# Nine run borders interleaved, and one weight conversion moved ahead, in a one-core two-model kernel

## The reference

```
h = rms_norm(x, g)
r, k, v, gate = (h + dx * mu[i]) @ w_in[i]          # i = 0..3, each 1024 x 1024
y = delta_rule_scan(r, decay, k, v, kk, a)          # state of 64 x 64 per head
x = x + (group_norm(y) + bonus) * silu(gate) @ w_out
x = x + sigmoid(rms_norm(x) @ w_gate0) * (p[0] @ w_proj0)
q, k, v, gate = rms_norm(x) @ da_w_in               # then softmax attention, 8 heads
x = x + (attention * silu(gate)) @ da_w_out
x = x + sigmoid(rms_norm(x) @ w_gate1) * (p[1] @ w_proj1)
b, c, xin, g = rms_norm(rms_norm(x)) @ w_in_a       # b * conv(c * xin) * silu(g)
x = x + conv_out @ w_out_a
...                                                 # stick-breaking attention, output norm
```

## Time and profile before

| what | value |
|---|---|
| median of the runs | 1260.31 us (1258.64 to 1261.17) |
| the profiled execution: its time, its span | 1260.45 us, 1258.7 us |
| TensorE matmuls busy | 1165.2 us, 93% |
| VectorE, ScalarE, GpSimd busy | 752.7, 617.9, 484.8 us |
| mean granted TensorE clock | 0.973 of full |

### The profile page before, as it was taken

The page is one execution under the profiler, slowest core; times in us unless marked ns, Lnnn a source line. Parts: engine busy times, 40 slices in busy tenths (PEclk is TensorE's granted clock), DMA queues, the critical chain, the costliest instruction groups (busy, mean ns, idle before and its releaser), DMA issues.

```text
span 1258.7 us, 19508 instructions
## 1 busy us (share of the span) xinstructions
PE 1165.2 (93%) x7570; PEld 901.6 (72%) x7570; DVE 752.7 (60%) x1179; ACT 617.9 (49%) x1018; POOL 484.8 (39%) x391
## 2 busy tenths in 40 slices
PE   5899899997886899899999998999999999999977
PEld 4665667676773687677777776777888888867656
DVE  4775996793556536566766656364285234567753
ACT  4667453633553336656656464364221244466655
POOL 1432334355760244323333334443444445532321
PEclk8999899998998899999999999999999999999988
DMA  6742245427005162221221222522333333222111
GB/s 235 251 113 67 68 102 149 131 88 194 12 4 172 34 191 85 84 67 56 77 67 55 67 84 68 165 86 69 99 100 90 96 100 101 84 76 60 52 33 67
DMA packets 198909, 119.49 MB, mean 95 GB/s; under 512 B 27741, under 2 KB 187174, under 8 KB 198566
## 3 DMA queue, kind: packets, MB, share of 16 engines
q1 hardware_dynamic: 197312, 116.08, 31.4%
q10 hardware_dynamic: 1510, 2.20, 0.5%
HBM read 103.06 MB, written 15.20 MB: 94 GB/s over the span
## 4 chain that ended last, share of the span: by engine, by line
PE 38%; issue 29%; POOL 15%; DVE 12%; ACT 2%; DMA 2%; SPq 0%; POOLq 0%; ACTq 0%; DVEq 0%
POOL b_w_lo L547 13%; PE banks L625 10%; PE banks L626 10%; PE banks L627 10%; DVE b_problems L2077 2%; DVE b_sum_squares L2075 1%; PE banks L1193 1%; DVE b_a_lo L1937 1%; PE banks L632 1%; PE banks L1221 1%; POOL b_sum_squares L592 1%; DVE b_sum_squares L2010 1%; DMA b_spread_heads<-spread_heads 1%; DVE b_suffix L2523 1%; POOL b_squares L584 1%
## 5 line engine op out<-in xcount | busy, mean ns | idle before, releaser
L547 POOL TENSOR_TENSOR b_w_lo<-b_w_raw,b_w_hi 128x512 fp32r<-128x512 f32 x320 | 428.9, 1361 | 717.3 <-ACT b_w_hi L1291 717.2
L625 PE MATMUL banks<-b_a_lo,b_w_hi 128*128 128x512 f32 x1280 | 525.0, 410 | 31.6 <-DVE b_a_lo L2190 12.7
L627 PE MATMUL banks<-b_a_hi,b_w_lo 128*128 128x512 f32 x1280 | 505.5, 395 | 0.0
L626 PE MATMUL banks<-b_a_hi,b_w_hi 128*128 128x512 f32 x1280 | 504.7, 394 | 0.0
L625 PEld LDWEIGHTS banks<-b_a_lo,b_w_hi 128*128 128x128 f32 x1280 | 243.8, 190 | 110.5 <-issue 26.1
L1291 ACT ACTIVATE b_w_hi<-b_w_raw 128x1024 fp32r<-128x1024 f32 x160 | 168.7, 1055 | 252.4 <-PE banks L627 247.0
L627 PEld LDWEIGHTS banks<-b_a_hi,b_w_lo 128*128 128x128 f32 x1280 | 243.7, 190 | 53.9
L626 PEld LDWEIGHTS banks<-b_a_hi,b_w_hi 128*128 128x128 f32 x1280 | 244.6, 191 | 44.6
L1682 ACT ACTIVATE b_exps<-banks,b_stats 128x128 f32<-128x128 f32 (+3 forms) x64 | 33.2, 524 | 60.1 <-DVE b_stats L2313 60.1
L1617 ACT ACTIVATE b_a_hi<-b_x_t,b_params 128x512 fp32r<-128x512 f32 x48 | 33.9, 719 | 54.7 <-DVE b_x_t L2198 54.2
L2198 DVE TENSOR_TENSOR b_x_t<-b_x_t,banks 128x512 f32<-128x512 f32 x32 | 21.9, 686 | 60.7 <-PE banks L627 60.7
(11 more groups left out here) (315 smaller groups left out, 1512.4 us busy)
## 6 DMA issues: line engine op xcount, KB each, us to landing
b_w_raw<-rw_w_in SPq DMA_DIRECT2D x32, 512.0 KB, 4.4
b_w_raw<-da_w_in SPq DMA_DIRECT2D x32, 512.0 KB, 4.0
b_w_raw<-w_in_a SPq DMA_DIRECT2D x32, 512.0 KB, 4.0
b_w_raw<-pe_w_gate SPq DMA_DIRECT2D x16, 512.0 KB, 4.1
d_ple<-b_ple_out SPq DMA_DIRECT2D x16, 256.0 KB, 4.9
b_w_raw<-rw_w_out SPq DMA_DIRECT2D x8, 512.0 KB, 6.6
b_ple_in<-d_ple SPq DMA_DIRECT2D x2, 2048.0 KB, 10.3
b_w_raw<-da_w_out SPq DMA_DIRECT2D x8, 512.0 KB, 4.0
```

The costliest lines, as they stand in the source:

```text
L547: m = pool.tensor_tensor(WLO[:, u % 2, ks], WRAW[:, u, ks], WHI[:, u % 2, ks].bitcast(F32), ALU.subtract)
L625: pe.matmul(dst, hi, a_lo[:, k_act, :], start=first, stop=False)
L626: pe.matmul(dst, hi, a_hi[:, k_act, :], start=False, stop=False)
L627: return pe.matmul(dst, lo, a_hi[:, k_act, :], start=False, stop=last)
```

## The change

At nine borders the order of TensorE's work is changed. Before, the first tile of a run is computed whole, then the second. After, the last `late` steps of the first tile stand behind the first `lead` steps of the second. What the second tile's first matmul waits for (`begin`) is waited for at its new place. The nine borders are v (late 4, lead 4), gate (2, 3), RWO (3, 5), PE0 (1, 2), DA (1, 2), DAO (2, 4), PE1 (1, 2), CC (1, 2) and CO (1, 2). Where there is a row norm, `sums` stays behind the first tile's last step and `spread` stays three steps behind `sums`. On ScalarE the high part of the third tile of DA, `hi(RUN_DA[0] + 2)`, is moved from ahead of the first rotation to ahead of the copy of `b_rstd`. No instruction is added or removed; VectorE's, GpSimd's and SyncE's programs are the same.

```
+        def rw_first_two(run, late, lead):
+            s = run * NT
+            rw_begin(s)
+            rw_part(s, 0, NT - late)
+            rw_begin(s + 1)
+            rw_part(s + 1, 0, lead)
+            rw_part(s, NT - late, NT)
...
+                rw_first_two(2, 4, 4)
...
+                rw_first_two(3, 2, 3)
...
+        def run_of(run, a0, buf, tiles=NT, norm=None, late=1, lead=2):
...
+            begin(0)
+            part(0, 0, NT - late)
+            begin(1)
+            part(1, 0, lead)
+            part(0, NT - late, NT)
+            if norm is not None:
+                norm[0]()
+                part(1, lead, lead + 3)
+                norm[1]()
+                part(1, lead + 3, NT)
...
+        run_of(RUN_RWO, A_RWO, 0, late=3, lead=5)
         run_of(RUN_PE0, A_PE0, 1, norm=norm_rows(16, 4))
...
+        DA_SWAPPED = {NT - 1: (1, 0), NT: (1, 1), NT + 1: (0, NT - 1)}
...
-        run_of(RUN_DAO, A_DAO, 1)
+        run_of(RUN_DAO, A_DAO, 1, late=2, lead=4)
...
         rows_root(3, TT)
+        hi(RUN_DA[0] + 2)
         keep_rstd(RB[:, :], 3, BANK[4])
...
-            if q == 1:
+            if q == 1 and p:
                 hi(g0 + 3 * p + 2)
```

More of the change, by code:

```diff
@@ L729, in rw_slot, with rw_part @@
             pe.wait_ge(sem(name), s - 3 - first if s >= 4 else s + 1)
-            for k in range(NT):
+        def rw_part(s, first, last, middle=None):
+            run, j = divmod(s, NT)
+            for k in range(first, last):
                 if j == 0:
                     pe.wait_ge(sem("act_ready"), A_K + NT * run + k + 1)
-                last = split_product(BANK[s % 4], s % 2, lambda w, k=k: w[:, k, :], k, k == 0, k == NT - 1)
+                m = split_product(BANK[s % 4], s % 2, lambda w, k=k: w[:, k, :], k, k == 0, k == NT - 1)
                 if j == NT - 1 and k < NT - 1:
-                    last.then_inc(sem("a_free"), 1)
+                    m.then_inc(sem("a_free"), 1)
                 if k == 3 and middle is not None:
                     middle()
-            last.then_inc(sem("mm_done"), 1)
+                if k == NT - 1:
+                    m.then_inc(sem("mm_done"), 1)
+        def rw_slot(s, middle=None):
+            rw_begin(s)
+            rw_part(s, 0, NT, middle)
+        def rw_first_two(run, late, lead):
+            s = run * NT
+            rw_begin(s)
+            rw_part(s, 0, NT - late)
+            rw_begin(s + 1)
+            rw_part(s + 1, 0, lead)
+            rw_part(s, NT - late, NT)
         low, up = slice(0, CH), slice(CH, P)
@@ L835, in _ @@
         for j in range(NT):
-            rw_slot(2 * NT + j)
+            if j == 0:
+                rw_first_two(2, 4, 4)
+            elif j == 1:
+                rw_part(2 * NT + 1, 4, NT)
+            else:
+                rw_slot(2 * NT + j)
             if j < 2:
@@ L848, in _ @@
         for j in range(NT):
-            rw_slot(3 * NT + j)
+            if j == 0:
+                rw_first_two(3, 2, 3)
+            elif j == 1:
+                rw_part(3 * NT + 1, 3, NT)
+            else:
+                rw_slot(3 * NT + j)
             if j == 0:
@@ L1012, in _ @@
             head_spread(BANK[4 + j % 4], SPREADHR2, RKC2, j).then_inc(sem("gn_bcast"), 1)
[L1013 to L1018, removed]
-            else:
[L1020 to L1035, removed]
+        def run_of(run, a0, buf, tiles=NT, norm=None, late=1, lead=2):
+            def begin(j):
+                pe.wait_ge(sem("lo_done"), run[0] + j + 1)
+                if run == RUN_DAO and j < 3:
+                    pe.wait_ge(sem("bank_free"), RUN_DAO[1] - (1 if j == 0 else 0))
+                else:
+                    pe.wait_ge(sem("bank_free"), run[1] + j - 3)
+            def part(j, first, last):
+                for k in range(first, last):
+                    if j == 0:
+                        pe.wait_ge(sem("act_ready"), a0 + k + 1)
+                    m = split_product(BANK[j % 4], (run[0] + j) % 2, lambda w, k=k: w[:, k, :], k, k == 0, k == NT - 1, buf)
+                    if k == NT - 1:
+                        m.then_inc(sem("mm_done"), 1)
+            begin(0)
[8 more added lines that the diff above has]
+                part(1, lead + 3, NT)
+            else:
+                part(1, lead, NT)
+            for j in range(2, tiles):
+                begin(j)
+                part(j, 0, NT)
```

9 lines of the change are left out of this document (4 added, 5 removed).

## The result

The changed kernel takes 1276.82 us, the median of four runs (1275.36 to 1280.79), against 1260.74 us before in the same session. The ratio is 1.0137, with a 95% interval of 1.0115 to 1.0160: slower by 1.4%, close to the forecast of 1274.0 us and well inside its range. The profiled execution took 1276.94 us with a span of 1275.2 us and a mean granted clock of 0.968.

What follows compares the result with a forecast made beforehand. TensorE is busy 93% of the span; after borders, later tiles wait for weights made from the first tile's end. 1260.45 + 7.4 (order) + 6.35 (clock) = 1274.2, forecast as 1274.0 us; range 1264 to 1281.

Steps and rivals of the forecast that it cites:

- the order's term: Delay from the reordering itself, border by border: PE0 +2.05, DAO +2.9, PE1 +2.1, CO +0.45, v -0.2; all borders +7.4 us.
- those on `sums`: Sign: `sums` of PE0 and PE1 start two steps later, behind a wait for the weights' low part (L547).
- on DAO's sixth step: Sign: DAO's sixth step is followed by 2 us idle for the weights' low part (L547).
- on the totals: Sign: TensorE's total waits for L547 grow by over 8 us while those for `b_a_lo` shrink.
- on the slow windows: Sign: the profile after has more windows at half clock.
- 3 to 4 us: Sign: the third tiles of RWO and DAO wait this long for the weights' low part (L547).
- Rival A: The waits move but the clock does not answer: only +7.4, 1267.7 us; chance 0.17.
- D: Rival: no change, delays at PE0, PE1, DAO absorbed by norm slack and the moved conversion; 1260 us, chance 0.05.
- C: Rival: faster, TensorE's own work sets the pace after a border, decided at RWO's and DAO's third tiles; 1252.6 us, chance 0.08.
- Net for the rotation, the rope and so `scores`: At DA: `sums` 0.65 later, conversion of 1.04 moved out from ahead of the rotation, net -0.4 us.
- it stays: At RWO: the way from first tile to third, 5.96 us, is unchanged; the border costs +0.5 us.
- CC's "0": At CC: the third tile still starts when its weights are ready, so 0 delay, with a wait of about 2.3 us.

Runs made afterwards that it cites:

- DAO alone: The kernel before with only DAO's border interleaved (late 2, lead 4): 1264.42 us, ratio 1.0032.
- RWO's shorter lead: The changed kernel with RWO at 3 late and 2 lead steps instead of 5 lead: 1274.09 us.
- hi first: In RWO and DAO, hi of the tile two on ahead of the residual wait: 1254.66 us on the kernel before, 1267.75 us on the changed kernel.
- the filled pauses: The changed kernel with unread matmuls in the waits at RWO, PE0, PE1, the scores and CC: 1268.63 us, ratio 1.0066.
- the one with the held high part: The changed kernel, where ScalarE makes the high part of DA's fifth tile only behind the first head's last rope addition: 1277.33 us.
- the two combined versions: The kernel before with hi first, RWO 3 late/2 lead, earlier high parts at PE, DA, CC: 1258.36 us; plus 20 unread matmuls: 1253.39 us.

## Why the prediction came out

The direction and the main mechanism were right: a later tile's weights hang on the first tile's end, and steps put between only delay that end. At PE0, DAO, PE1, CO and before RWO the order's term came within 0.2 us. Undoing PE0 and PE1, DAO alone and RWO's shorter lead show the mechanism from three sides; hi first shows that the pace was the chain and names its slack link. Of the signs named beforehand those on `sums`, on DAO's sixth step, on the totals and on the slow windows are in the profile after; the waits of 4.21 and 2.93 us ahead of RWO's and DAO's third tiles lie just outside the "3 to 4 us", and PE0's fourth tile waits 2.44 us instead of 1.11. Rival A (no clock) and D (no change) are out by the filled pauses and by DAO alone; C fell with 4.21 us of wait ahead of RWO's third tile.

Two steps failed, both for the same reason: they followed the moved work on its own chain and not what then runs beside it. The first is "Net for the rotation, the rope and so `scores`". It holds to the rope (-0.34 for -0.4). But the conversion moved on ScalarE also lets the conversions behind it, and so a GpSimd subtraction, come 0.5 us earlier against the rope, and VectorE's last addition meets it: +0.92 us. The second is RWO's "it stays", and CC's "0". From the first tile's residual addition to the third tile's start RWO took 428.47 - 422.82 = 5.65 us before and 429.22 - 423.08 = 6.14 us after, since VectorE's split of the second tile now delays the subtraction; the same cost CC 0.46 us.

The order term so was 9.1 for 7.4, with 0.4 more spread over the rest, and the clock term 7.0 for 6.35. The price of one stretch, 1.7 us, was near (1.5 to 1.6). That the clock's sum came out so near is luck: the three pauses counted by half (measured 2.43 to 2.63 us) all got a stretch, and DAO's, counted in full, none. The Trainium skill's page "TensorE: Matmul & The Clock Gate", section "HAM oscillation — how this bites in real kernels", has every long enough wait answered by the slow clock; five of six were so here, and DAO's wasn't. The sum by that rule, about 1278, lies nearer to 1276.8 than mine, but for no better reason: its clock term, 10.2, is 3.2 too large, and the order term in it is 2.1 too small.

## What to carry to other kernels

Work put into a wait is worth something only if what the wait holds up isn't also held up by what was moved; follow the first late thing behind the border (here the third tile's weights) back to where it starts, and shorten that chain instead. ScalarE's conversions in two runs, placed ahead of a wait that they don't need, gave 6 us, where nine reordered borders cost 16. When an instruction moves, follow also the engine that it feeds, and look for what that one now runs beside.

## What the runs showed of the hardware

The same pause doesn't get the same clock: 2.57 us ahead of DA's third tile was followed by 1.00 before, and by 0.50 with hi first (timeline and window of that trace):

```profile
524.56 0.50 PE L625 MATMUL banks<-b_a_lo,b_w_hi 128*128 128x512 f32 x1 [2.57 <-POOL b_w_lo L547]
```

```profile
525.30:528.50 3.20, 3.20 (x10) 2.46 (x9) 2.09 (x2) 1.11 (x3) 2.98 (x2) 0.50 0.57 164
```

The traces of all kernels here give a count for these places. Behind a pause of 2.93 us at DAO's third tile the clock fell in three of six (DAO alone, the filled one and the one with the held high part), behind one of 2.43 or 2.44 us at the fourth tiles of PE0 and PE1 in six of eight, and behind one of 4.21 us in RWO or of 4.7 to 6.0 us at the scores in all ten. What decides between the two for the shorter ones isn't shown.

Kernels with the same code in their first 60 us came out of it up to 3.3 us apart (the two combined versions), and stretches at half rate moved a total by 2 to 3 us where nothing had been edited. An effect of 1 us must therefore be read between two places of a trace, not from a median.

Matmuls that nobody reads are a remedy: 61 of them took 8.2 us off the changed kernel. A VectorE addition of 128 x 512 with both inputs in SBUF can take 1.63 us instead of 0.69 when a GpSimd subtraction begins 0.2 us ahead of it. And the GpSimd subtraction takes 1.80 us instead of 1.29 when such a VectorE instruction began 0.08 us ahead of it.
